# Local attention's probabilities turned by VectorE squares and a trip through device memory, instead of by TensorE transposes

## The chip, the cores and the metric

The kernel runs on one core of a Trainium2 chip. The metric is device time in microseconds of one execution. It is compared as the median of several runs.

## The reference

Two transformer blocks run on 512 tokens of width 1024, all in fp32. The change touches one piece of the first block, the local attention beside the matrix LSTM:

```python
def sliding_window_attention(q, k, v, sinks, rel_bias):
    ...
    logits = jnp.einsum('bnqhgd,bnkhd->bnhgqk', qb, kb).astype(f32) * (SWA_HEAD_DIM ** -0.5)
    ...
    mx = jnp.maximum(logits.max(-1, keepdims=True), sink)
    p = jnp.exp(logits - mx)
    probs = (p / (p.sum(-1, keepdims=True) + jnp.exp(sink - mx))).astype(v.dtype)
    out = jnp.einsum('bnhgqk,bnkhd->bnqhgd', probs, vb)
```

There are 8 heads of 64 with 2 key/value heads, and query blocks of 128 that see their own 128 keys and the 128 before (the first block sees only its own). Behind it come the output projection, cross attention over 256 memory tokens, a convolutional feed-forward net, a second block with four mixers, and its MLP.

## The kernel before

**The weights.** Every large product multiplies fp32 values split into two fp32r halves: hi by hi, lo by hi, and hi by lo, so three matmuls for one. Weights arrive in chunks of 128 x 1024 (512 KB). SyncE issues each chunk's load into one of three `stage` buffers (L2729). ScalarE casts it to `whi` (L1699), VectorE subtracts to `wlo` (L2176), and there are six places for split chunks. SyncE issues the load of chunk i+3 once VectorE has split chunk i, and the cast of a chunk waits until TensorE has used the chunk six before it.

**The order.** A class `Plan` writes the order of all steps out by hand. Every engine goes through the same list `plan.steps` and does its own part of each step, so each engine's order follows the list. `fill` takes the next free one of 8 PSUM banks, first in, first out, and `out` gives a bank back with the semaphore that frees it.

**The stage around the change.** While the first block's feature products run (`in_a`, 17 chunks, then `kv_k`, 8 chunks), small work is slipped between them by `beside_mixer_one` (L349). That is a generator: each `yield` stands for about half a chunk of feature products, 12 matmuls of 128x512 (or 24 of 128x256 further on). The local attention is cut into eight units u (two head pairs by four query blocks; units 0 and 4 have one key block, the others two), each with four heads:

- `swa_score(u)`: TensorE makes the logits in two banks (L1525). VectorE scales them, adds the bias into `L[u % 3]` (L2287), takes the negative maximum (L2291, L2293) and starts the sink's exponent (L2295).
- `swa_exp(u)`: ScalarE's exponentials with row sums (L1794). VectorE adds the sink and takes the reciprocal (L2299, L2301).
- `swa_norm(u)`: ScalarE multiplies by it (L1803).
- `swa_turn(u)`: TensorE transposes the probabilities in squares of 128x128 (L1539), 8 per unit and 4 in units 0 and 4. ScalarE copies the banks into `PTs[u % 2]` (L1814, L1816).
- `swa_pv(u)`: TensorE multiplies by the values (L1551, two records for each fp32 matmul). ScalarE copies the result to `hT` (L1821).

The mLSTM's steps follow: `ml_gate` (L1559), `ml_score` (L1566), `ml_out` (L1580). `mem_load` (L2761) loads the memory tokens, `mem_in` (L1719, L2202) splits them, and `kv_k` multiplies them. On SyncE, `mem_load` stands between the weight chunks.

## Time and profile before

| | us |
|---|---|
| median of 3 runs | 1285.17 (1284.91 to 1285.43) |
| span of the profiled execution | 1282.5 |
| TensorE busy in it | 1275.4 |
| VectorE busy | 728.4 |
| ScalarE busy | 576.5 |
| mean granted TensorE clock | 0.999 |

The span runs from the first to the last instruction of the profiled execution. That execution has no time of its own on the page, so its span is set beside the median: 2.7 us of the 1285.17 lie outside it. Busy time counts overlapping matmuls once. A matmul's duration is its latency, and the distance between two starts is what it takes from the engine.

### The profile page before, as it was taken

The page shows a single profiled execution, that of the slowest core. Times are in us where ns is not written, and L with a number is a line of the kernel's source. Part 1 is how long each engine was busy: PE and PEld are TensorE (multiplying, and loading weights), DVE is VectorE, ACT ScalarE, POOL GpSimd, SP SyncE. Part 2 cuts the span into 40 slices and gives each one's busy share as a digit, 9 for nine tenths or more (in the row PEclk, how much of TensorE's full clock was granted, in tenths as well). Part 3 has the DMA queues.
Part 4 walks back from the last instruction along what each step waited for, and adds up shares of the span by engine and source line. Part 5 has one row for each costly group of instructions (what it writes and reads, how often), then busy time and mean ns, then how long its engine had stood idle before and what let it go on. Part 6 is the DMA issues. An engine that isn't in the chain of part 4 may idle for free.

```text
span 1282.5 us, 16066 instructions
## 1 busy us (share of the span) xinstructions
PE 1275.4 (99%) x6462; PEld 1071.2 (84%) x6462; DVE 728.4 (57%) x1083; ACT 576.5 (45%) x988; POOL 7.0 (1%) x8
## 2 busy tenths in 40 slices
PE   9999999999999999999999999999999999999998
PEld 9877898898889888888888898778898888888886
DVE  5767678475576555555533489777653433433333
ACT  5577644245446444444522364576432422322222
POOL 0000001000000000000000000000000000000000
PEclk9999999999999999999999999999999999999999
DMA  8421245322234333333433142123243233333311
GB/s 257 142 78 66 99 132 157 138 54 79 82 99 132 99 99 99 99 99 99 148 99 99 33 152 92 57 66 115 64 151 93 92 97 97 115 99 99 99 50 66
DMA packets 38145, 131.20 MB, mean 102 GB/s; under 512 B 4372, under 2 KB 5908, under 8 KB 37816
## 3 DMA queue, kind: packets, MB, share of 16 engines
q1 hardware_dynamic: 37640, 129.79, 32.3%
q8 instruction: 51, 0.84, 0.3%
q10 hardware_dynamic: 432, 0.39, 0.1%
q14 instruction: 22, 0.18, 0.1%
HBM read 128.07 MB, written 2.10 MB: 101 GB/s over the span
## 4 chain that ended last, share of the span: by engine, by line
PE 99%; DMA 0%; DVE 0%; ACT 0%; issue 0%; DVEq 0%
PE bank L1283 18%; PE bank L1284 18%; PE bank L1285 18%; PE bank L1424 5%; PE bank L1425 5%; PE bank L1428 5%; PE bank L1429 5%; PE bank L1426 5%; PE bank L1427 5%; PE bank L1503 1%; PE bank L1580 1%; PE bank L1566 1%; PE bank L1366 1%; PE bank L1355 1%; PE bank L1525 1%; PE bank L1405 1%
## 5 line engine op out<-in xcount | busy, mean ns | idle before, releaser
L1283 PE MATMUL bank<-xh,whi 128*128 128x512 f32 (+1 forms) x1136 | 414.7, 365 | 0.0
L1285 PE MATMUL bank<-xh,wlo 128*128 128x512 f32 (+1 forms) x1136 | 409.9, 361 | 0.0
L1284 PE MATMUL bank<-xl,whi 128*128 128x512 f32 (+1 forms) x1136 | 409.9, 361 | 0.0
L2176 DVE TENSOR_TENSOR wlo<-stage,whi 128x1024 fp32r<-128x1024 f32 (+1 forms) x222 | 267.5, 1211 | 226.3 <-ACT whi L1699 226.1
L1699 ACT CAST whi<-stage 128x1024 fp32r<-128x1024 f32 (+1 forms) x222 | 228.5, 1036 | 198.1 <-PE bank L1429 157.1
L1283 PEld LDWEIGHTS bank<-xh,whi 128*128 128x128 f32 x1136 | 214.4, 189 | 37.6 <-issue 5.5
L1285 PEld LDWEIGHTS bank<-xh,wlo 128*128 128x128 f32 x1136 | 214.4, 189 | 32.8
L1284 PEld LDWEIGHTS bank<-xl,whi 128*128 128x128 f32 x1136 | 214.5, 189 | 31.7 <-issue 0.2
L1424 PE MATMUL bank<-whi,xh 128*128 128x512 f32 x281 | 110.3, 393 | 0.1
L1425 PE MATMUL bank<-whi,xh 128*128 128x512 f32 x281 | 109.4, 389 | 0.0
L1429 PE MATMUL bank<-whi,xl 128*128 128x512 f32 x281 | 109.4, 389 | 0.0
L1426 PE MATMUL bank<-wlo,xh 128*128 128x512 f32 x281 | 109.4, 389 | 0.0
L1427 PE MATMUL bank<-wlo,xh 128*128 128x512 f32 x281 | 109.3, 389 | 0.0
L1428 PE MATMUL bank<-whi,xl 128*128 128x512 f32 x281 | 109.3, 389 | 0.0
L2702 DVE TENSOR_TENSOR R<-bank,R 128x512 f32<-128x512 f32 x32 | 22.1, 692 | 90.7 <-ACT R L2145 90.7
L2145 ACT ACTIVATE R<-bank 128x512 f32<-128x512 f32 x32 | 19.1, 598 | 113.4 <-PE bank L1285 113.4
L2508 DVE SCALAR_TENSOR_TENSOR R<-R,par 128x512 f32<-128x512 f32 x44 | 33.1, 752 | 60.5 <-ACT R L1937 60.5
L1934 ACT COPY R<-bank 128x512 f32<-128x512 f32 x44 | 25.8, 587 | 83.7 <-PE bank L1285 83.7
L1424 PEld LDWEIGHTS bank<-whi,xh 128*128 128x128 f32 x281 | 52.8, 188 | 11.1 <-issue 0.5
L1427 PEld LDWEIGHTS bank<-wlo,xh 128*128 128x128 f32 x281 | 52.8, 188 | 11.1
L1428 PEld LDWEIGHTS bank<-whi,xl 128*128 128x128 f32 x281 | 52.7, 188 | 11.0
L1429 PEld LDWEIGHTS bank<-whi,xl 128*128 128x128 f32 x281 | 52.8, 188 | 10.9
(341 smaller groups left out, 1413.0 us busy)
## 6 DMA issues: line engine op xcount, KB each, us to landing
stage<-in_W_m SPq DMA_DIRECT2D x64, 512.0 KB, 3.6
stage<-in_W_up SPq DMA_DIRECT2D x44, 512.0 KB, 3.6
stage<-in_W_down SPq DMA_DIRECT2D x22, 512.0 KB, 3.6
stage<-in_W_in_a SPq DMA_DIRECT2D x19, 512.0 KB, 4.1
stage<-in_W_out SPq DMA_DIRECT2D x16, 512.0 KB, 3.7
stage<-in_W_in_b SPq DMA_DIRECT2D x10, 512.0 KB, 3.6
stage<-in_W_kv_k SPq DMA_DIRECT2D x8, 512.0 KB, 3.3
stage<-in_W_kv_v SPq DMA_DIRECT2D x8, 512.0 KB, 4.1
```

Source lines behind the costliest of these rows:

```text
L1283: e.matmul(b[:, cols], hi[:, k, :], xh[:, k, cols], start=(k == 0), stop=False)
L1284: e.matmul(b[:, cols], hi[:, k, :], xl[:, k, cols], start=False, stop=False)
L1285: last = e.matmul(b[:, cols], lo[:, k, :], xh[:, k, cols], start=False, stop=(k == 7))
L1424: e.matmul(b[0][:], a_hi, hi[:, 0:512], start=(k == 0), stop=False)
L1425: e.matmul(b[1][:], a_hi, hi[:, 512:1024], start=(k == 0), stop=False)
L1426: e.matmul(b[0][:], a_hi, lo[:, 0:512], start=False, stop=False)
L1427: e.matmul(b[1][:], a_hi, lo[:, 512:1024], start=False, stop=False)
L1428: e.matmul(b[0][:], a_lo, hi[:, 0:512], start=False, stop=end)
L1429: return e.matmul(b[1][:], a_lo, hi[:, 512:1024], start=False, stop=end)
L1699: e.copy(whi[:, plan.place[i], 0:width(i)], stage[:, s, 0:width(i)]).then_inc(S["w_hi"])
L2176: e.tensor_tensor(wlo[:, plan.place[i], c], stage[:, i % NSTAGE, c], whi[:, plan.place[i], c].bitcast(F32), ALU.subtract).then_inc(S["w_lo"])
L2508: e.scalar_tensor_tensor(out=y, in0=u[:, 0:512], scalar=P("fcw", w), in1=y, op0=ALU.mult, op1=ALU.add).then_inc(own.inc())
```

## The change

The transposes leave TensorE. In their place VectorE turns each unit's probabilities in squares of 32x32 (one instruction per unit, from `L` into row 2 of `gb`, in which keys four apart come to stand side by side). SyncE stores the 128x1024 (128x512 in units 0 and 4) to a scratch tensor in device memory, waits until the store has landed, waits for the values' product of the unit two before, and loads it back into `PTs[u % 2]` with runs of 1 KB (512 B in units 0 and 4), which puts the squares into place. ScalarE's copies from PSUM go. The values' product reads its moving operand in runs of 32 elements. The fills of PSUM banks by `swa_turn` go, and several steps move in the list:

```diff
-SWA_BANKS = [1, 2, 2, 2, 1, 2, 2, 2]
...
+        self.step("swa_turn", 4)
         self.step("swa_exp", 5)
         yield
-        self.swa_turn(4)
         self.step("swa_norm", 5)
+        self.swa_score(6)
+        yield
+
         self.swa_pv(3)
-        self.swa_score(6)
-        yield
-
+        self.step("swa_turn", 5)
         self.step("swa_exp", 6)
         yield
-        self.swa_pv(4)
         self.step("swa_norm", 6)
         self.swa_score(7)
         yield
 
-        self.swa_turn(5)
+        self.swa_pv(4)
+        self.step("swa_turn", 6)
         self.step("swa_exp", 7)
         yield
         self.step("swa_norm", 7)
         yield
-
-        self.swa_turn(6)
+        self.step("swa_turn", 7)
         self.step("mem_load")
         self.ml_gate(0)
         yield
+        self.swa_pv(5)
         self.step("ml_exp", 0)
         yield
 
-        self.swa_pv(5)
+        self.ml_score(0)
+        yield
         self.swa_pv(6)
-        self.swa_turn(7)
-        self.ml_score(0)
-        yield
-        yield
-
-        self.swa_pv(7)
+        yield
+
         self.ml_gate(1)
         yield
         self.step("ml_exp", 1)
         self.ml_out(0)
         yield
 
+        self.swa_pv(7)
         self.ml_score(1)
```

On TensorE the values' product changes:

```diff
-                q.wait_ge(S["swa_pt"], sum(SWA_BANKS[:u + 1]))
+                q.wait_ge(s_turned[u % 2], 16 * (u // 2 + 1))
                 q.wait_ge(S["sv_out"], 4)
                 kbs = [0, 1] if n else [1]
-                for kb in kbs:
+                P = swa_turned(u)
+                for z, kb in enumerate(kbs):
                     for j in range(2):
                         last = e.matmul(b[64 * j:64 * j + 64, 0:256], swv[:, n - 1 + kb, 64 * j:64 * j + 64],
-                                        PTs[u % 2][:, j, kb, :], start=(kb == kbs[0]), stop=(kb == 1))
+                                        P[:, j, z, :, :, :], start=(kb == kbs[0]), stop=(kb == 1))
...
+        def swa_turned(u):
+
+            k = 2 if u % 4 else 1
+            v = PTs[u % 2][:, 0:512 * k]
+            return v.rearrange("p (b j i k c) -> p j k i b c", b=4, j=2, i=2, k=k)
```

New on VectorE (first) and on SyncE (second):

```diff
+            def swa_turn(u):
+
+                q.wait_ge(S["swa_p"], u + 1)
+                if u:
+                    q.wait_ge(S["swa_out"], 16 * u)
+                else:
+                    q.wait_ge(S["gate_h"], 1)
+                    q.wait_ge(S["gate_l"], 2)
+                m = 8 if u % 4 else 4
+                src = L[u % 3].rearrange("p g (k a r) -> p r g k a", k=2, r=4)
+                dst = blocks[:, 0:128 * m]
+                if m == 8:
+                    e.transpose(dst.rearrange("p (r g k a) -> p r g k a", r=4, g=4, k=2), src).then_inc(S["swa_tr"])
+                else:
+                    e.transpose(dst.rearrange("p (r g a) -> p r g a", r=4, g=4), src[:, :, :, 1, :]).then_inc(S["swa_tr"])
...
+            def swa_turn(u):
+                w = 1024 if u % 4 else 512
+                q.wait_ge(S["swa_tr"], u + 1)
+                e.dma_start(turned[u][:, 0:w], blocks[:, 0:w]).then_inc(S["swa_out"], 16)
+                q.wait_ge(S["swa_out"], 16 * u + 16)
+                if u >= 2:
+                    q.wait_ge(S["swa_o_full"], u - 1)
+                e.dma_start(PTs[u % 2][:, 0:w].rearrange("p (b c) -> p b c", b=4),
+                            turned[u][:, 0:w].rearrange("(b a) (r c) -> (a r) b c", b=4, r=4)).then_inc(s_turned[u % 2], 16)
```

Waits elsewhere for the transposes (`swa_t_full`) now wait for VectorE's squares (`swa_tr`), and `ml_out(0)` on VectorE no longer waits for the last values' product.

How the instructions move, at three places. On TensorE, before, around unit 3's product (L1539 transposes, L1551 values' product, L1525 scores; each x4 of L1551 is one unit with two key blocks, x2 one with one, and between the groups stand the feature products, L1283 to L1285):

```order
L1285 MATMUL bank<-xh,wlo 128x512
L1539 MATMUL bank<-ident,R 128x128 x4
L1551 MATMUL bank<-R 64x256 x4
L1525 MATMUL bank<-R 128x256 x4
L1283 MATMUL bank<-xh,whi 128x512
...
L1551 MATMUL bank<-R 64x256 x2
L1525 MATMUL bank<-R 128x256 x4
L1283 MATMUL bank<-xh,whi 128x512
```

Now (L1527 scores, L1540 values' product, L1285 to L1287 features):

```order
L1527 MATMUL bank<-R 128x256 x4
L1285 MATMUL bank<-xh,whi 128x512
...
L1540 MATMUL bank<-R 64x256 x4
L1285 MATMUL bank<-xh,whi 128x512
...
L1527 MATMUL bank<-R 128x256 x4
L1285 MATMUL bank<-xh,whi 128x512
...
L1540 MATMUL bank<-R 64x256 x2
```

Twelve feature matmuls stand between each of these and the next: the group of unit 4's transposes, unit 3's product and unit 6's scores has become two groups, with no transposes, and so has unit 4's product with unit 7's scores.

On VectorE, before, between the scores of unit 2 and the next conv, with the semaphores that each waits for:

```order
L2293 TENSOR_TENSOR st<-st,gb 128x4 [waits v_own]
L2295 TENSOR_TENSOR st<-gb,st 128x4 [waits swa_nm]
L2318 SCALAR_TENSOR_TENSOR R<-R 128x512 [waits qk_t]
L2176 TENSOR_TENSOR wlo<-stage,whi 128x1024 [waits w_hi,st0]
L2299 TENSOR_TENSOR st<-st 128x4 [waits swa_e]
```

Now:

```order
L2270 TENSOR_TENSOR st<-st,gb 128x4 [waits v_own]
L2272 TENSOR_TENSOR st<-gb,st 128x4 [waits swa_nm]
L2292 STREAM_TRANSPOSE gb<-R 128x1024 [waits swa_out,swa_p]
L2311 SCALAR_TENSOR_TENSOR R<-R 128x512 [waits qk_t]
L2153 TENSOR_TENSOR wlo<-stage,whi 128x1024 [waits w_hi,st2]
L2276 TENSOR_TENSOR st<-st 128x4 [waits swa_e]
```

Unit 1's squares stand behind unit 2's logits and ahead of a silu and a chunk's split. On SyncE, before:

```order
L2729 DMA stage<-in_W_in_a 128x1024 [waits w_lo] x10
L2729 DMA stage<-in_W_kv_k 128x1024 [waits w_lo] x6
L2761 DMA R<-in_memT 128x2048 [waits swa_s_full]
```

Now, from the last units on:

```order
L2760 DMA turned<-gb 128x1024
L2764 DMA R<-turned 128x4x256
L2723 DMA stage<-in_W_kv_k 128x1024
L2760 DMA turned<-gb 128x1024
L2764 DMA R<-turned 128x4x256
L2755 DMA R<-in_memT 128x2048
L2723 DMA stage<-in_W_kv_k 128x1024 x2
```

Sixteen transfers stand between the weight chunks, the last two directly ahead of the memory tokens' load.

## Rows read from the trace of the kernel before

**Rows 1.** The page: busy us of each engine, its share of the span and its instructions.
```profile
PE 1275.4 (99%) x6462; PEld 1071.2 (84%) x6462; DVE 728.4 (57%) x1083; ACT 576.5 (45%) x988; POOL 7.0 (1%) x8
```

**Rows 2.** The longest of TensorE's waits (engine line <- releaser: us in total, times, longest us).
```profile
PE bank L1678 <- DVE R L2224: 1.2, 1, 1.2
```

**Rows 3.** TensorE's timeline (start us, us, engine, line, ...), around unit 1's transposes.
```profile
78.63 0.39 PE L1285 MATMUL bank<-xh,wlo 128*128 128x512 f32 x1
78.86 1.03 PE L1539 MATMUL bank<-ident,R 128*128 128x128 f32 x8
79.65 0.48 PE L1283 MATMUL bank<-xh,whi 128*128 128x512 f32 x1
79.97 0.40 PE L1284 MATMUL bank<-xl,whi 128*128 128x512 f32 x1
```

**Rows 4.** TensorE's timeline, around the transposes of units 0 and 4.
```profile
68.92 0.60 PE L1539 MATMUL bank<-ident,R 128*128 128x128 f32 x4
69.59 0.40 PE L1284 MATMUL bank<-xl,whi 128*128 128x512 f32 x1
...
112.13 0.60 PE L1539 MATMUL bank<-ident,R 128*128 128x128 f32 x4
112.66 1.08 PE L1551 MATMUL bank<-R 128*64 128x256 f32 x8
```

**Rows 5.** TensorE's timeline, units 5 and 6's products, unit 7's transposes.
```profile
138.48 1.95 PE L1551 MATMUL bank<-R 128*64 128x256 f32 x16
140.36 1.09 PE L1539 MATMUL bank<-ident,R 128*128 128x128 f32 x8
141.29 2.32 PE L1566 MATMUL bank<-R 128*128 128x512 f32 x8
```

**Rows 6.** TensorE's timeline, in and out of a short group between feature products.
```profile
149.08 0.28 PE L1285 MATMUL bank<-xh,wlo 128*128 128x256 f32 x1
149.29 1.08 PE L1551 MATMUL bank<-R 128*64 128x256 f32 x8
...
150.73 0.38 PE L1283 MATMUL bank<-xh,whi 128*128 128x256 f32 x1
150.95 0.28 PE L1284 MATMUL bank<-xl,whi 128*128 128x256 f32 x1
```

**Rows 7.** Groups by form (xcount | busy us, mean ns | idle before).
```profile
L1539 PE MATMUL bank<-ident,R 128*128 128x128 f32 x56 | 7.5, 273 | 0.0
...
L2291 DVE TENSOR_REDUCE st<-R 128x4 f32<-128x1024 f32 x6 | 7.3, 1220 | 0.2
```

**Rows 8.** Timelines: unit 1 normed, unit 2's logits done, product 1; the latter for product 0.
```profile
70.04 1.71 ACT L1803 ACTIVATE R<-R,st 128x256 f32<-128x256 f32 x4
...
78.58 0.17 DVE L2295 TENSOR_TENSOR st<-gb,st 128x4 f32<-128x4 f32 x1
...
93.51 1.08 PE L1551 MATMUL bank<-R 128*64 128x256 f32 x8
...
66.24 0.16 DVE L2295 TENSOR_TENSOR st<-gb,st 128x4 f32<-128x4 f32 x1
...
82.56 0.65 PE L1551 MATMUL bank<-R 128*64 128x256 f32 x4
```

**Rows 9.** DMA issues (xcount, KB each, median us from issue to landing).
```profile
stage<-in_W_in_a SPq DMA_DIRECT2D x19, 512.0 KB, 4.1
...
R<-in_x SPq DMA_DIRECT2D x4, 512.0 KB, 7.4
...
out<-R SPq DMA_DIRECT2D x3, 512.0 KB, 2.6
```

**Rows 10.** Window of the squares: PE, PEld, DVE, ACT, POOL busy (x), clock, DMA share, GB/s.
```profile
66.40:134.40 68.00, 68.00 (x353) 52.27 (x352) 45.27 (x80) 49.60 (x131) 0.00 (x0) 1.00 0.22 70
```

**Rows 11.** Timelines: the memory tokens' cast, the group ahead of their first product.
```profile
146.58 2.00 ACT L1719 CAST xh<-R 128x1024 fp32r<-128x1024 f32 x2 [4.45 <-PE bank L1285]
...
153.71 2.40 PE L1580 MATMUL bank<-R 128*128 128x129 f32 x20
```

More of the change, by code:

```diff
@@ L308, in swa_score @@
         self.step("swa_score", u)
-    def swa_turn(self, u):
-        for z in range(SWA_BANKS[u]):
-            self.fill("swa_turn", u, z)
-            self.out(("swa_turn", u, z), "swa_pt", sum(SWA_BANKS[:u]) + z + 1)
-        self.step("swa_turn", u)
     def swa_pv(self, u):
@@ L361, in beside_mixer_one @@
         yield
+        self.step("swa_turn", 0)
         self.step("swa_exp", 1)
         yield
-        self.swa_turn(0)
         self.step("swa_norm", 1)
@@ L370, in beside_mixer_one @@
         yield
+        self.step("swa_turn", 1)
         self.step("swa_exp", 2)
         yield
-        self.swa_turn(1)
         self.step("swa_norm", 2)
@@ L379, in beside_mixer_one @@
         yield
+        self.step("swa_turn", 2)
         self.step("swa_exp", 3)
         yield
-        self.swa_turn(2)
         self.step("swa_norm", 3)
@@ L389, in beside_mixer_one @@
         yield
+        self.step("swa_turn", 3)
         self.step("swa_exp", 4)
         yield
-        self.swa_turn(3)
         self.step("swa_norm", 4)
@@ L1141, in build_program @@
         L = [tiles(reg(kb, 1024), 4) for kb in (24, 72, 68)]
-        PTs = [reg(76 + 4 * i, 1024).rearrange("p (j k c) -> p j k c", j=2, k=2) for i in range(2)]
+        PTs = [reg(76 + 4 * i, 1024) for i in range(2)]
+        blocks = gb[:, 2, :]
+        s_turned = [S["swa_in0"], S["swa_in1"]]
         vaug = reg(84, 2064).rearrange("p (t h c) -> p t h c", t=4, h=4)
@@ L1263, in bank_of @@
             return bank[plan.bank[key][0]]
+        turned = [nc.dram_tensor(f"turned{u}", (128, 1024 if u % 4 else 512), F32, kind="Internal").ap() for u in range(8)]
         block = ctx.enter_context(nc.Block())
@@ L1527, in swa_score @@
                 last.then_inc(S["swa_s_full"])
-            def swa_turn(u):
-                n = u % 4
-                q.wait_ge(S["ld_c"], 32)
-                q.wait_ge(S["swa_p"], u + 1)
-                for j in range(2):
-                    if j < SWA_BANKS[u]:
-                        b = fill("swa_turn", u, j)
-                    for kb in ([0, 1] if n else [1]):
-                        a = kb * 256 if n else j * 256
-                        for i in range(2):
-                            last = e.transpose(b[:, a + 128 * i:a + 128 * i + 128], L[u % 3][:, 2 * j + i, tok(kb)], ident[:])
-                    if j or SWA_BANKS[u] == 2:
-                        last.then_inc(S["swa_t_full"])
             def swa_pv(u):
@@ L1804, in swa_norm @@
                 last.then_inc(S["swa_p"])
-            def swa_turn(u):
-                m = sum(SWA_BANKS[:u])
-                if u >= 2:
-                    q.wait_ge(S["swa_o_full"], u - 1)
-                for z in range(SWA_BANKS[u]):
-                    q.wait_ge(S["swa_t_full"], m + z + 1)
-                    b = bank_of("swa_turn", u, z)
-                    if SWA_BANKS[u] == 2:
-                        e.copy(PTs[u % 2][:, z, :, :], tiles(b[:], 2)).then_inc(S["swa_pt"])
-                    else:
-                        e.copy(PTs[u % 2][:, :, 1, :], tiles(b[:], 2)).then_inc(S["swa_pt"])
             def swa_pv(u):
@@ L1846, in ml_exp @@
                 q.wait_ge(S["ml_d"], h + 1)
-                q.wait_ge(S["swa_t_full"], sum(SWA_BANKS[:6 + 2 * h]))
+                q.wait_ge(S["swa_tr"], min(8, 6 + 2 * h))
                 if h >= 2:
@@ L1867, in kv_v @@
                 q.wait_ge(S["qk_s"], 8)
-                q.wait_ge(S["swa_t_full"], sum(SWA_BANKS))
+                q.wait_ge(S["swa_tr"], 8)
                 e.copy(VM[:, t, hf * 512:(hf + 1) * 512], bank_of("kv_v", hf, t)[:]).then_inc(S["vm_out"])
@@ L2282, in swa_score @@
                 if u >= 3:
-                    q.wait_ge(S["swa_t_full"], sum(SWA_BANKS[:u - 2]))
+                    q.wait_ge(S["swa_tr"], u - 2)
                 q.wait_ge(S["swa_s_full"], u + 1)
@@ L2354, in ml_out @@
                 q.wait_ge(S["ml_h_full"], h + 1)
-                q.wait_ge(S["swa_t_full"], sum(SWA_BANKS))
-                q.wait_ge(S["swa_o_full"], 8)
+                q.wait_ge(S["swa_tr"], 8)
+                if h:
+                    q.wait_ge(S["swa_o_full"], 7)
                 for z in range(2):
@@ L2810, in _ @@
                 x_load(k)
-            mine = dict(begin=begin, bias_load=bias_load, split=split, x_in=x_in, consts=consts, mem_load=mem_load, x_again=x_again, rows=rows, mix2_loads=mix2_loads, store=store)
+            mine = dict(begin=begin, bias_load=bias_load, split=split, x_in=x_in, consts=consts, mem_load=mem_load, swa_turn=swa_turn, x_again=x_again, rows=rows, mix2_loads=mix2_loads, store=store)
             for name, *a in plan.steps:
```

18 lines of the change are left out of this document (9 added, 9 removed).

## Prediction

> **What bounds the kernel now.** I read the page's busy shares first, then TensorE's waits, then the timelines of the stretch in which the local attention runs. TensorE is busy for 1275.4 of the 1282.5 us of the span [rows 1], and its longest wait is 1.2 us, once, at the start [rows 2]. So TensorE's own instruction stream is the time, and every other engine is cover. Only two things can move the time: an instruction that leaves or joins that stream, or a wait that did not exist. The span stands 2.7 us under the median of 1285.17; I take the differences below as the same in both.
>
> **What leaves TensorE.** The transposes are listed with 273 ns each [rows 7]. That is a latency: the eight of unit 1 start at 78.86 and the next product starts at 79.65, so they take 0.79 us, 0.1 each. The first product behind them takes 0.32 us to the next start instead of the usual 0.23 (78.63 to 78.86), so a lone group of eight costs 79.97 - 78.86 - 0.23 = 0.88 us [rows 3]. Units 1, 2, 3, 5 and 6 are of this kind: 5 x 0.88 = 4.4 us. Unit 0 (four transposes): 69.59 - 68.92 - 0.23 = 0.44 us. Unit 4 stands ahead of a values' product: 112.66 - 112.13 = 0.53 us, less the 0.09 us that a product behind feature matmuls pays to get in (149.08 + 0.12 = 149.20, start at 149.29 [rows 6]), so 0.44 [rows 4]. Unit 7, in the middle of a group: 141.29 - 140.36 = 0.93 us [rows 5]. Sum removed: 4.4 + 0.44 + 0.44 + 0.93 = 6.2 us.
>
> The Trainium skill, "TensorE: Matmul & The Clock Gate", section "Part 4: PE-mode transpose", gives a transpose about 275 ns in a kernel. The trace's duration agrees (273), but its starts are 0.1 us apart, and the starts decide; by 275 ns each the sum would be 15 us.
>
> **What the reordering adds to TensorE.** Each short group between feature products costs 0.09 us to get in and 0.10 to get out (150.73 to 150.95 is 0.22 where a half product takes 0.12) [rows 6]. The groups on transposes alone go, and that is in the sum above. But product 3 now stands apart from scores 6, product 4 from scores 7, and the large group of products 5 and 6 with the first mLSTM scores becomes three. That is four groups more: 4 x 0.19 = 0.8 us. Product 7 only changes the group that it is part of.
>
> **The values' product itself** keeps its number of records and columns, but reads its moving operand in runs of 32 elements instead of 128. No row shows such an operand. The trace's product reads contiguous columns: 16 records take 1.88 us (138.48 to 140.36 [rows 5]) and 8 take about 1.0 with the change of kind behind them, so one is 0.11 us. Bounds: 0 if runs of 32 stream as well, and 56 x 0.11 = +6.2 us if they halve the rate. I take 0, nearest to the contiguous row, because the elements still lie side by side for 32 starts in a row.
>
> **Sum:** -6.2 + 0.8 = -5.4 us, to 1279.8.
>
> **What must be hidden for that.** Three pieces of new work lie on engines that are cover now.
>
> *VectorE* gets eight square turns, six of 1024 columns. No row shows a transpose there. The nearest row by size is the reduce over 1024 columns, 1.22 us [rows 7]. Lower end: half of that, 0.6 us; upper end: double, 2.4 us, because the source is read with a stride of four elements. I take 1.2 for 1024 columns and 0.7 for 512, so 8.6 us in all; at the upper end it is 17. In the window in which they fall VectorE is busy for 45.3 of 68.0 us [rows 10], so 22.7 us are idle, and both fit. ScalarE loses 14 copies in the same window. The turn waits for ScalarE's norm, but that is early: for unit 1 it ends at 71.75, and VectorE comes to the place of the turn at 78.75, behind unit 2's logits [rows 8]. What queues behind the turn is a silu, a chunk's split and the next reciprocal. They come 1.2 us later, and a chunk is split six places ahead of its use.
>
> The Trainium skill, "SBUF — State Buffer", section "Door 1: The DMA port swizzle", says that compute engines read 16-byte lines and pay for each step to another line; here every source element is on a new line. That rule speaks for the upper end, and for the product's runs of 32, which use every line fully, it speaks for 0. No run here has shown either.
>
> *The trip.* The product of unit u must find both transfers done. Unit 1 is the tightest. VectorE reaches the turn at 78.75 and TensorE reaches product 1 at 93.51 [rows 8], 14.8 us later. The transposes of units 1 and 2 leave TensorE in between (-1.8), and the turn takes 1.2, so 11.8 us are left for store and load. Unit 0 has 82.56 - 66.40 = 16.2, less 1.3 and 0.7, so 14.1; units 2 and 4 come out near 14 in the same way, and the rest, whose products moved back or which have a free yield, above 15. The nearest rows: a store of 512 KB lands in 2.6 us, and a load of 512 KB in 4.1 among the weight chunks; the slowest load of that size took 7.4, behind others [rows 9]. So the pair is 6.7 us and at most 2 x 7.4 = 14.8. By 6.7 nothing waits, with 5 us to spare at unit 1. By 14.8 unit 1 waits 3.0 us and units 0, 2 and 4 about 0.7 each: +5.
>
> *SyncE's queue.* SyncE waits for each store to land before it goes on, and the weight chunks stand behind it. It loses the store's 2.6 us (at most 7.4) per unit, while a chunk's load is issued three chunks ahead of its cast. A chunk is 24 products of 0.23 us, 5.5 us, so the lead is 16 us less 4.1 to land: 12 us. It holds. The last pair stands ahead of the memory tokens' load. Their cast waits for TensorE until 146.58, and their first product comes after the group at 153.71 [rows 11], so the load can be some 5 us late without cost. The extra bytes are under 7 MB in a window with a DMA share of 0.22 [rows 10].
>
> **Rivals.**
>
> *A. The trip is too long (slower).* The products 0 to 7 wait in TensorE's stream for a load whose store first has to land in device memory. It decides from a pair of 11.8 us on. Because everything hangs on TensorE, a wait does not give the next unit more room. At 18 us units 1, 0, 2 and 4 wait 6.2, 3.9, 3.8 and 3.9 us, and the other four about 2 each: 26 us, to 1306; at 16 us it is about 10 us, to 1290. SyncE's chunks starve from the same point. For it: each unit has two transfers in a row, with a wait on SyncE between, and the load is cut into runs of 1 KB, which no row of that size shows. Against it: the rows of 2.6 and 4.1 us. I give 0.08, at 1290.
>
> *B. Small waits.* The pair is 12 to 15 us at one or two units, or VectorE at 2.4 us per turn comes late to a bank or a split. TensorE waits 1 to 5 us: 1281 to 1285. For it: VectorE and ScalarE work in step here and each late piece is passed on. I give 0.10.
>
> *C. The strided operand halves the product's rate.* +6.2 us on the forecast, 1286.0: the gain is spent where it was made. Chance 0.06.
>
> *D. The listed duration is what a transpose costs.* Then 56 x 0.273 = 15.3 us leave, less 0.8: 1270.7. Against it are the starts of rows 3, 0.1 us apart. Chance 0.02. It is also the time by the skill's 275 ns.
>
> **How the numbers follow.** A measurement of this kernel tells a change of 0.2% (2.6 us) from none, so faster is below 1282.6. My forecast, 1279.8, has 0.74, and a range of its own from 1278.0 (the split groups cost nothing and the removed transposes leave all of the 6.2 us, with a run's spread) to 1281.5. B adds 0.10 up to 1284.8. So the range of 1278.0 to 1284.8 holds 0.84 and leaves out A, C and D. Faster: 0.74, D's 0.02 and half of B, so 0.81. Same: the other half of B and C, which ends 0.8 us above the time before, so 0.11. Slower: A, 0.08.
>
> **What would show it.** In the changed profile TensorE has 56 transpose records fewer on the attention's line and, if I am right, no wait of its own at the values' product. The product's records still start 0.11 us apart inside a group (0.22 would be C). A square turn on VectorE lasts near 1.2 us (2.4 is the stride's price). Store and load together land within 7 us of the turn's end and SyncE's chunks still wait for VectorE's splits. The prediction is wrong if TensorE waits for a load of `PTs`, or for a bank or a split in the stretch from 65 to 160 us, by more than 1 us in all, or if the time changes anywhere behind that stretch, where no instruction has changed.

## The result, and the profile after

The change makes the kernel faster: median 1281.45 us (1280.76 to 1281.67, 7 runs) against 1284.98 (1284.82 to 1285.43, 7 runs) for the kernel before, a ratio of 0.997 with a 95% interval of 0.9961 to 0.9979. That is 3.5 us where 5.4 were forecast. It lies inside the range and on the side that was forecast; 1.9 us of the gain are missing.

The page of the kernel after: its span, each engine's busy time (as [rows 1]) and the chain that ended last, by engine.

```profile
span 1279.3 us, 15979 instructions
PE 1271.2 (99%) x6406; PEld 1065.5 (83%) x6406; DVE 740.7 (58%) x1091; ACT 569.1 (44%) x974; POOL 7.0 (1%) x8
PE 92%; DVE 4%; ACT 2%; DMA 1%; issue 1%; DVEq 0%; SPq 0%
```

TensorE has 56 records fewer and is busy for 4.2 us less than in [rows 1]; the span is 3.2 us shorter. What TensorE waited for (us in total, times, longest us), as [rows 2], says where some of the gain went:

```profile
PE bank L1667 <- DVE R L2201: 1.2, 1, 1.2
PE bank L1285 <- DVE xl L2179: 0.9, 1, 0.9
PE bank L1322 <- ACT xh L1695: 0.2, 1, 0.2
```

The first is the wait that was there before. The second is new: the first product of the memory tokens (L1285) waits for VectorE's split of them (L2179). No wait for `PTs` at the values' product (L1540) is listed. The same list for TensorE's weight loads (PEld) has, beside the same wait for the split, one at 157.63 for a PSUM bank that VectorE gives back with its work on the mLSTM outputs (L2363):

```profile
PEld bank L1285 <- DVE R L2363: 0.5, 1, 0.5
```

(A third, of 0.35 us at 121.54, is no longer than the gap that weight loads have ahead of such a group in any case.) The kernel before has no wait for another engine in the attention's stretch.

The square turns and one TensorE form, by source line (xcount, shortest, median and longest ns, first and last start, form):

```profile
L2292 DVE STREAM_TRANSPOSE gb<-R x6: 1983/2005/2054, 78.5 to 133.9; 128x1024 f32<-128x1024 f32 x6
...
L2294 DVE STREAM_TRANSPOSE gb<-R x2: 1080/1086/1093, 68.5 to 110.3; 128x512 f32<-128x512 f32 x2
...
L1540 PE MATMUL bank<-R x56: 379/379/430, 81.7 to 154.8; 128*64 128x256 f32 x56
```

A turn takes 2.0 us, nearer the upper bound of 2.4 than the 1.2 taken. The values' product keeps its duration, and eight of its records still take 1.08 us [rows 6], so runs of 32 elements cost it nothing.

The trip's transfers in the list of DMA issues (xcount, KB each, median us from issue to landing), beside [rows 9]:

```profile
turned<-gb SPq DMA_DIRECT2D x6, 512.0 KB, 3.1
R<-turned SPq DMA_DIRECT2D x6, 512.0 KB, 3.9
...
turned<-gb SPq DMA_DIRECT2D x2, 256.0 KB, 3.4
R<-turned SPq DMA_DIRECT2D x2, 256.0 KB, 2.7
```

So a store and a load take 7.0 us in the median, near the 6.7 of the sum.

**Where the time is.** I compare starts of the same TensorE groups, counted from the first scores, because the start-up ahead of them differs from one execution to the next (52.41 us before, 52.91 after; more on this below). Up to the first mLSTM output group (L1580, 153.71 before [rows 11]; L1569, 147.72 after), TensorE is (153.71 - 52.41) - (147.72 - 52.91) = 6.49 us ahead. Product 7, 1.02 us, now stands behind that point, so 5.47 us have been gained there: the forecast's 5.4. Behind it the gain shrinks. TensorE's timeline after (start us, us, engine, line):

```profile
147.72 2.40 PE L1569 MATMUL bank<-R 128*128 128x129 f32 x20
...
151.01 0.39 PE L1285 MATMUL bank<-xh,whi 128*128 128x256 f32 x1 [0.89 <-DVE xl L2179]
...
154.07 1.08 PE L1540 MATMUL bank<-R 128*64 128x256 f32 x8
155.09 2.42 PE L1555 MATMUL bank<-R 128*128 128x512 f32 x8
```

What stood in front of that wait, on ScalarE and then on VectorE:

```profile
147.44 1.99 ACT L1708 CAST xh<-R 128x1024 fp32r<-128x1024 f32 x2 [5.69 <-DMA R<-in_memT]
```
```profile
132.71 1.23 DVE L2153 TENSOR_TENSOR wlo<-stage,whi 128x1024 fp32r<-128x1024 f32 x1 [0.32 <-ACT whi L1688]
133.86 2.05 DVE L2292 STREAM_TRANSPOSE gb<-R 128x1024 f32<-128x1024 f32 x1
...
148.59 2.36 DVE L2179 TENSOR_TENSOR xl<-R,xh 128x1024 fp32r<-128x1024 f32 x2 [3.92 <-ACT xh L1708]
```

And SyncE's queue, the first line from the kernel before, the others after:

```profile
134.85 0.43 SPq L2761 DMA_DIRECT2D R<-in_memT  x1
```
```profile
131.81 0.37 SPq L2764 DMA_DIRECT2D R<-turned  x1
133.97 0.33 SPq L2723 DMA_DIRECT2D stage<-in_W_kv_k  x1
135.94 0.32 SPq L2760 DMA_DIRECT2D turned<-gb  x1
140.86 0.37 SPq L2764 DMA_DIRECT2D R<-turned  x1
141.28 0.51 SPq L2755 DMA_DIRECT2D R<-in_memT  x1
```

Read backwards: the product at 151.01 waited for VectorE's split, which waited for ScalarE's cast, which had stood idle for 5.69 us until the memory tokens' load landed at 147.4. Before, the same cast was held up by TensorE instead ([rows 11]). The load was issued at 141.28, because SyncE first waited for unit 7's store: issued at 135.94, right behind unit 7's turn (133.86 + 2.05), and waited for until 140.86, 4.9 us. In the kernel before, the load was issued at 134.85.

The second wait follows from the first. VectorE splits the memory tokens from 148.59 on, where e1_mem_first below has it do so from 145.45 on, so its work on the mLSTM outputs comes late too. The second piece of it ends at 157.22 + 0.35 = 157.57, and the next feature product starts at 157.63, 2.54 us behind the start of the mLSTM scores instead of 2.08.

### The profile page after: what moved, and what is told of

Read it like the earlier page. It is cut to its first block, busy times and chain, and to the rows that moved or that the text cites. A ratio compares the mean times of both kernels' runs of the same rounds, so it can differ in the third digit from the quotient of the medians.

```text
span 1279.3 us, 15979 instructions
## 1 busy us (share of the span) xinstructions
PE 1271.2 (99%) x6406; PEld 1065.5 (83%) x6406; DVE 740.7 (58%) x1091; ACT 569.1 (44%) x974; POOL 7.0 (1%) x8
## 2 busy tenths in 40 slices
DMA packets 43521, 138.54 MB, mean 108 GB/s; under 512 B 4628, under 2 KB 10260, under 8 KB 43192
## 4 chain that ended last, share of the span: by engine, by line
PE 92%; DVE 4%; ACT 2%; DMA 1%; issue 1%; DVEq 0%; SPq 0%
PE bank L1285 16%; PE bank L1286 16%; PE bank L1287 16%; PE bank L1426 5%; PE bank L1427 5%; PE bank L1429 5%; PE bank L1430 5%; PE bank L1428 5%; PE bank L1431 5%; PE bank L1505 1%; DVE wlo L2153 1%; DVE R L2302 1%; PE bank L1357 1%; PE bank L1368 1%; DVE gb L2292 1%
## 5 line engine op out<-in xcount | busy, mean ns | idle before, releaser
L1285 PE MATMUL bank<-xh,whi 128*128 128x512 f32 (+1 forms) x1136 | 414.6, 365 | 1.0 <-DVE xl L2179 0.9
L1287 PE MATMUL bank<-xh,wlo 128*128 128x512 f32 (+1 forms) x1136 | 409.9, 361 | 0.0
L1285 PEld LDWEIGHTS bank<-xh,whi 128*128 128x128 f32 x1136 | 214.4, 189 | 40.8 <-issue 7.0
L1287 PEld LDWEIGHTS bank<-xh,wlo 128*128 128x128 f32 x1136 | 214.4, 189 | 32.5
L1429 PEld LDWEIGHTS bank<-wlo,xh 128*128 128x128 f32 x281 | 52.7, 188 | 11.1
L1428 PEld LDWEIGHTS bank<-wlo,xh 128*128 128x128 f32 x281 | 52.8, 188 | 11.1
L1431 PEld LDWEIGHTS bank<-whi,xl 128*128 128x128 f32 x281 | 52.7, 188 | 11.0
```

What stands on the lines that cost most here:

```text
L1285: e.matmul(b[:, cols], hi[:, k, :], xh[:, k, cols], start=(k == 0), stop=False)
L1287: last = e.matmul(b[:, cols], lo[:, k, :], xh[:, k, cols], start=False, stop=(k == 7))
L1428: e.matmul(b[0][:], a_hi, lo[:, 0:512], start=False, stop=False)
L1429: e.matmul(b[1][:], a_hi, lo[:, 512:1024], start=False, stop=False)
L1431: return e.matmul(b[1][:], a_lo, hi[:, 512:1024], start=False, stop=end)
```

## The experiments

I call the explanation so far theory L: the load of the memory tokens stands behind unit 7's trip and lands too late; that costs the wait and the lateness behind it. Its rivals: VectorE's longer turns cost the time in themselves, by making later pieces late; the groups that the new order splits off cost more than the 0.19 us that the sum counts for each; the trips hold up SyncE's weight chunks. The number that I compare in each is the *stretch*, from the first scores to the start of the last group of mLSTM transposes (L1587 before, L1576 after), because it leaves out the start-up: 220.61 - 52.41 = 168.20 us before and 217.38 - 52.91 = 164.47 after. Of the 5.47 us gained at 147.72, 3.73 are left there. Its two ends, before and then after:

```profile
52.41 0.71 PE L1525 MATMUL bank<-R 64*128 64x128 f32 x8
...
220.61 0.60 PE L1587 MATMUL bank<-ident,R 128*128 128x128 f32 x4
```
```profile
52.91 0.72 PE L1527 MATMUL bank<-R 64*128 64x128 f32 x8
...
217.38 0.60 PE L1576 MATMUL bank<-ident,R 128*128 128x128 f32 x4
```

Behind the stretch nothing changed: the stretch is 3.7 us shorter, and the 0.5 us more in front of it leave the 3.2 us between the spans. Each stretch is read from the one profiled execution of its kernel.

**e1_mem_first: the memory tokens' load ahead of the last trip.**

```diff
-        self.step("swa_turn", 7)
         self.step("mem_load")
+        self.step("swa_turn", 7)
         self.ml_gate(0)
```

> The change, with the memory tokens' load issued on SyncE ahead of unit 7's store and load instead of behind them; nothing else moves. Theory L (of the forecast's 5.4 us, some 1.6 are lost because that load is issued 6 us late, behind a store that SyncE waits for): TensorE's 0.9 us wait at the first kv_k product goes and so does the half microsecond that follows in the first mLSTM score group behind it; 1.4 to 1.8 us less than the change, near 1279.8. Rival V (VectorE's turns of 2.0 us instead of 1.2 are what is late, and the load only stands there): at most 0.3 us less. Rival N (the half microsecond by which this execution is behind before the attention begins is part of the change, not spread): the start of the first scores stays at 52.9 here too; as spread it varies between 52.4 and 52.9.

Measured: 1280.45 us (1280.10 to 1280.75) against 1284.79 for the kernel before, ratio 0.9964 (0.995 to 0.9977). TensorE's waits no longer name the split:

```profile
PE bank L1667 <- DVE R L2201: 1.2, 1, 1.2
PE bank L1322 <- ACT xh L1695: 0.2, 1, 0.2
```

The load is issued at 135.20 and the stretch is 162.92 us, 5.28 less than before and 1.55 less than in the change. Product 7 starts 5.20 us behind the mLSTM output group instead of 6.35, and the group behind it lasts 8.11 us to the next anchor instead of 8.49. The turns still take 2.01 us. So the late load cost 1.15 us directly and 0.4 behind it, and the wait of the weight load for VectorE's bank is gone as well. This separates L from the rival on the turns, which expected at most 0.3 us. The length of the turns by itself costs nothing where the load does not hang on the last of them. The median gained only 4.3 us because this kernel's first scores start at 53.77 in the profiled execution, 1.36 us later than before: 5.28 - 1.36 is the 3.9 us between the spans (1282.5 and 1278.6).

**e2_contiguous_turn: the turn reads neighbouring elements.** ScalarE's copy of the keys, the bias and the mask put the keys in turned order, so that the square turn has no stride of four at its source.

```diff
-                e.copy(swk if j == 0 else swq[:, int(MIX1[j][2]), :], bank_of("in_a", j)[:]).then_inc(S["a_out"])
+                e.copy(swk.rearrange("p (t r a) -> p t a r", t=4, r=4) if j == 0 else swq[:, int(MIX1[j][2]), :],
+                       bank_of("in_a", j)[:].rearrange("p (t a r) -> p t a r", t=4, r=4) if j == 0 else bank_of("in_a", j)[:]
+                       ).then_inc(S["a_out"])
...
-                src = L[u % 3].rearrange("p g (k a r) -> p r g k a", k=2, r=4)
+                src = L[u % 3].rearrange("p g (k r a) -> p r g k a", k=2, r=4)
...
-    r, c = np.arange(128)[:, None], np.arange(256)[None, :]
+    r, c = np.arange(128)[:, None], np.arange(256).reshape(2, 32, 4).transpose(0, 2, 1).reshape(1, 256)
```

> The change, with the keys put in the turned order once, when ScalarE copies them from PSUM (and the bias and mask laid out so on the host), so that the square turn reads 32 elements side by side instead of a stride of four. If the stride is the price of the turn (2.0 us for 1024 columns), it falls to about 1.1; if a turn of fp32 costs that whatever the stride, it stays at 2.0. For the time: V expects 1.4 to 1.8 us less. L expects the same only as far as the last turn, and with it the memory tokens' load, comes earlier: one turn alone gives 0.9 us of the 1.1 us lost directly, several turns together more. If the duration stays, both expect no change.

Measured: 1280.08 us (1279.68 to 1280.65), ratio 0.9961 (0.9948 to 0.9973); stretch 162.93. The turn in the groups by form (xcount | busy us, mean ns | idle us before), first of e1_mem_first, whose source has the stride, then of e2_contiguous_turn:

```profile
L2292 DVE STREAM_TRANSPOSE gb<-R 128x1024 f32<-128x1024 f32 x6 | 12.1, 2012 | 0.0
...
L2294 DVE STREAM_TRANSPOSE gb<-R 128x512 f32<-128x512 f32 x2 | 2.2, 1081 | 0.0
```
```profile
L2294 DVE STREAM_TRANSPOSE gb<-R 128x1024 f32<-128x1024 f32 x6 | 7.4, 1239 | 0.0
...
L2296 DVE STREAM_TRANSPOSE gb<-R 128x512 f32<-128x512 f32 x2 | 1.4, 702 | 0.0
```

Without the stride a turn takes 1.24 us for 1024 columns and 0.70 for 512, just what the sum took (1.2 and 0.7). The stride costs 0.77 us per large turn. With turns that short the load of the memory tokens is issued at 140.28 instead of 141.28, and TensorE's wait is gone too. The last store is issued 2.2 us earlier (133.76 instead of 135.94), but it then takes 6.1 us instead of 4.9 (to 139.86), so only 1.0 us of that reaches the load. So the turn's length did cost time, by one way alone: through the load behind unit 7. This and e1_mem_first end at the same stretch, which speaks for one cause and not for two.

**e3_order_only: the new order, with TensorE's transposes kept.** From the kernel before, with the products at the change's places, and the wait of `ml_out(0)` on VectorE cut to match:

```diff
         self.swa_turn(4)
         self.step("swa_norm", 5)
-        self.swa_pv(3)
         self.swa_score(6)
         yield
+        self.swa_pv(3)
         self.step("swa_exp", 6)
         yield
-        self.swa_pv(4)
         self.step("swa_norm", 6)
         self.swa_score(7)
         yield
+        self.swa_pv(4)
         self.swa_turn(5)
...
         self.ml_gate(0)
         yield
+        self.swa_pv(5)
         self.step("ml_exp", 0)
         yield
-        self.swa_pv(5)
-        self.swa_pv(6)
         self.swa_turn(7)
         self.ml_score(0)
         yield
+        self.swa_pv(6)
         yield
-        self.swa_pv(7)
         self.ml_gate(1)
...
         self.ml_out(0)
         yield
+        self.swa_pv(7)
         self.ml_score(1)
...
-                q.wait_ge(S["swa_o_full"], 8)
+                if h:
+                    q.wait_ge(S["swa_o_full"], 7)
```

> The kernel before, with TensorE's transposes and ScalarE's copies kept, but the values' products at the places of the change (3 behind scores 6, 4 behind scores 7, 5, 6 and 7 apart). By the forecast's term each group more among the feature products costs 0.19 us; here there are three more (eight become eleven), so +0.6 us against the kernel before, within 0.2. If a group costs nothing, 0; if the moved products wait for something, over 1 us, and a wait of TensorE is listed.

Measured: 1285.99 us (1285.49 to 1286.98, 11 runs) against 1284.79, ratio 1.0008 (1.0 to 1.0017); stretch 169.19, 0.99 more than before. So the new order by itself gains nothing; it costs about 1 us of the stretch. Here it splits off three groups (product 4 stays with unit 5's transposes), so 3 x 0.19 = 0.6 us of the 0.99 were counted. Some 0.1 us is product 7 in its new group (8.11 us to the next anchor instead of 7.99), and 0.3 us stay unexplained; no wait is listed.

**e4_trip_on_gpsimd: GpSimd issues the trips.** SyncE's part of `swa_turn` moves word for word to GpSimd, in a loop over the eight units, so that SyncE waits for no store.

```diff
+            for u in range(8):
+                swa_turn(u)
             for h in range(4):
...
-            mine = dict(begin=begin, bias_load=bias_load, split=split, x_in=x_in, consts=consts, mem_load=mem_load, swa_turn=swa_turn, x_again=x_again, rows=rows, mix2_loads=mix2_loads, store=store)
+            mine = dict(begin=begin, bias_load=bias_load, split=split, x_in=x_in, consts=consts, mem_load=mem_load, x_again=x_again, rows=rows, mix2_loads=mix2_loads, store=store)
```

> The change, with the store and load of the turned squares issued by GpSimd instead of SyncE, so that no weight chunk and not the memory tokens' load stands behind them. L expects the load to be issued near 134 us instead of 141, TensorE's 0.9 us wait to go, and 1.4 to 1.8 us less than the change, unless GpSimd's transfers take over 4 us longer than SyncE's, when a product of the values waits (0 to 3 us more). V expects at most 0.3 us less.

Measured: 1280.05 us (1279.58 to 1280.26), ratio 0.996 (0.9948 to 0.9973); stretch 162.92. The memory tokens' load is issued at 134.79, the wait is gone, and a store and a load take 3.1 and 4.3 us in the median. All that this edit frees beyond e1_mem_first is the weight chunks' loads, and the stretch is the same to 0.01 us: SyncE's chunks were never short.

**e5_mem_first_contiguous: both edits, e1's and e2's.**

```diff
-        self.step("swa_turn", 7)
         self.step("mem_load")
+        self.step("swa_turn", 7)
...
-                src = L[u % 3].rearrange("p g (k a r) -> p r g k a", k=2, r=4)
+                src = L[u % 3].rearrange("p g (k r a) -> p r g k a", k=2, r=4)
...
```

> Both mends at once: the memory tokens' load ahead of unit 7's trip, and the contiguous square turn. If the late load was all that was lost, the second mend has nothing left to give: the same as either alone within 0.2 us in the stretch from the first scores on, 1280.1 to 1280.5. If VectorE's time still costs TensorE something that no listed wait shows, another 0.5 us or more less.

Measured: 1280.10 us (median of five runs, 1279.08 to 1280.20; a sixth took 5816 us and is left out), ratio 0.9959 (0.9946 to 0.9972). The stretch is 162.92 us, as with either edit alone, although the load is now issued at 132.07. Two cures of one wait do not add up.

**e6_mem_first_store_twice: a longer trip, with the load out of its way.** From e1_mem_first, with each store made twice, one behind the other.

```diff
-                q.wait_ge(S["swa_out"], 16 * u + 16)
+                q.wait_ge(S["swa_out"], 32 * u + 16)
+                e.dma_start(turned[u][:, 0:w], blocks[:, 0:w]).then_inc(S["swa_out"], 16)
+                q.wait_ge(S["swa_out"], 32 * u + 32)
```

> The memory tokens' load first, and every unit's squares stored twice, the second store waiting for the first: each trip is one store longer, by about 3.1 us. In the trace of the change the loads land 3.8 to 9 us before their product (nearest for units 2 and 5). The forecast's term (a trip costs TensorE nothing below its slack) expects at most 0.5 us more than with the memory load alone first. Rival A (the trip is what TensorE hangs on) expects 8 times 3 us, 20 us or more.

Measured: 1280.42 us (1279.85 to 1281.50), ratio 0.9964 (0.9952 to 0.9975); stretch 163.69, 0.77 more than e1_mem_first. One wait appears, at product 7:

```profile
PE bank L1540 <- DMA R<-turned: 0.5, 1, 0.5
```

That is 0.3 us more than the 0.5 expected at most. Seven of the eight units still wait for nothing, although from the issue of the first store to the landing of the load they now take about 8 to 11 us. Unit 7's first store stands behind the memory tokens' load of 1 MB and takes 9.4 us by itself (138.00 to 147.41), and its trip some 16. So trips of that length cost nothing here, as the prediction said with its room of 11.8 us. The 16 and 18 us at every unit that rival A was priced for were not reached, so this run says nothing on its price.

**e8_store_twice: the same on the change itself**, with the memory tokens' load left behind the last trip. The diff is e6's, on the kernel after.

> The change with every unit's squares stored twice and the memory tokens' load left behind unit 7's trip. L expects that load, and TensorE's wait for it, to come about 3 us later: 3 to 3.5 us more than the change, near 1284.8, all of it at the first kv_k product. Without that place (the run with the memory load first) the same doubling should cost nothing.

Measured: 1287.32 us (1286.13 to 1288.32, 11 runs) against 1285.18, ratio 1.0018 (1.001 to 1.0027): slower than the kernel before. The stretch is 171.49 us, 7.0 more than the change, about twice what was expected. TensorE's wait for the split has grown from 0.9 to 6.0 us:

```profile
PE bank L1285 <- DVE xl L2179: 6.0, 1, 6.0
```

The last unit's two stores took 6.4 and 2.6 us (SyncE went on 143.24 - 136.85 and 145.82 - 143.24 later), and the load went out at 146.57 instead of 141.28. That is 5.3 later, and the wait is 5.1 longer; it agrees. The rest comes from the clock. Windows of TensorE around the wait, the busy time of PE, PEld, DVE, ACT and POOL (x instructions), the granted clock, the DMA share and GB/s:

```profile
149.90:155.90 6.00, 0.01 (x1) 0.00 (x0) 2.39 (x3) 3.54 (x5) 0.00 (x0) 0.87 0.46 188
155.90:158.00 2.10, 2.08 (x9) 2.08 (x10) 2.03 (x4) 2.08 (x6) 0.00 (x0) 0.50 0.00 0
158.00:160.00 2.00, 2.00 (x11) 2.00 (x11) 2.00 (x3) 2.00 (x7) 0.00 (x0) 0.50 0.00 0
160.00:162.00 2.00, 2.00 (x15) 1.60 (x14) 1.79 (x9) 0.80 (x1) 0.00 (x0) 0.72 0.17 35
162.00:164.00 2.00, 2.00 (x9) 0.97 (x6) 1.75 (x8) 0.00 (x0) 0.00 (x0) 1.00 0.61 236
```

After 6.0 us without work the granted clock is at 0.50, the 1.2 GHz level, until some time between 160 and 162 us. From the first product behind the wait to product 7, TensorE takes 5.35 us here and 3.06 in the change: 2.3 us on top of the wait. Behind product 7 it is 0.4 us faster than the change (62.92 us to the end of the stretch instead of 63.31): VectorE has caught up, and the wait for its bank is gone. 5.1 + 2.3 - 0.4 are the 7.0 us.

**e7_merged_groups: the split groups put together again.** From e5_mem_first_contiguous: product 3 with scores 6, 4 with 7, 5 with the first mLSTM scores, 6 with the second gate.

```diff
+        self.swa_pv(3)
         self.swa_score(6)
         yield
-        self.swa_pv(3)
...
+        self.swa_pv(4)
         self.swa_score(7)
         yield
-        self.swa_pv(4)
...
-        self.swa_pv(5)
         self.step("ml_exp", 0)
         yield
+        self.swa_pv(5)
         self.ml_score(0)
         yield
-        self.swa_pv(6)
         yield
+        self.swa_pv(6)
         self.ml_gate(1)
```

> Both mends, and the values' products put back into groups: 3 with scores 6, 4 with scores 7, 5 with the first mLSTM scores, 6 with the second gate. Four groups fewer among the feature products at 0.19 us each: 0.8 us less than both mends, near 1279.3, if the loads are there in time. Product 4 then stands 4 us earlier, with about 1 us of slack left; if it waits, up to 1 us of that is given back.

Measured: 1280.11 us (1279.15 to 1281.28), ratio 0.9959 (0.9947 to 0.9971); stretch 163.36, 0.44 more than e5_mem_first_contiguous. Product 4 now stands half a chunk and a group of scores earlier, and gets there 1.0 us before its load has landed:

```profile
PE bank L1540 <- DMA R<-turned: 1.0, 1, 1.0
```

Without that 1.0 us the four merges would have gained 0.56, 0.14 each.

**e9_merged_but_4: the same without the merge of product 4.**

> Both mends and the merged groups, but product 4 left where the change has it, behind scores 7. In the run with all groups merged product 4 waited 1.0 us for its load; without that wait the stretch from the first scores on would have been 0.6 us shorter than with both mends. Here no wait of TensorE, and 0.4 to 0.6 us less than both mends in that stretch; in the medians that is within their spread.

Measured: 1279.79 us (1279.03 to 1280.21) against 1285.05, ratio 0.9955 (0.9942 to 0.9969). The values' product waits for nothing, and the stretch is 162.50, 0.42 less than e5_mem_first_contiguous for three merges, again 0.14 each.

**e10_one_leg: no scratch memory.** All four merges, and four transfers from SBUF to SBUF per unit in place of the store and the load, each one reading 32 partitions and writing 128. Nothing waits for a store any more, and the next turn waits for these transfers instead.

```diff
-                e.dma_start(turned[u][:, 0:w], blocks[:, 0:w]).then_inc(S["swa_out"], 16)
-                q.wait_ge(S["swa_out"], 16 * u + 16)
                 if u >= 2:
                     q.wait_ge(S["swa_o_full"], u - 1)
-                e.dma_start(PTs[u % 2][:, 0:w].rearrange("p (b c) -> p b c", b=4),
-                            turned[u][:, 0:w].rearrange("(b a) (r c) -> (a r) b c", b=4, r=4)).then_inc(s_turned[u % 2], 16)
+                for b in range(4):
+                    e.dma_start(PTs[u % 2][:, b * w // 4:(b + 1) * w // 4],
+                                blocks[32 * b:32 * b + 32, 0:w].rearrange("a (r c) -> a r c", r=4)).then_inc(s_turned[u % 2], 16)
```

> All groups merged, both mends, and no scratch tensor: four transfers per unit, one for each 32 partitions of the turned squares, go from SBUF straight into place, so that SyncE waits for no store. If two legs are what made product 4 late, its load now lands 3 us earlier or more, the 1.0 us wait goes, and the stretch is 0.6 us shorter than with both mends, at or below the run with product 4 left apart. If a transfer from 32 partitions to 128 in runs of 1 KB is much slower than a load (over 7 us), product 4 waits as before or longer.

Measured: 1278.91 us (1278.73 to 1279.71) against 1285.05, ratio 0.9952 (0.9939 to 0.9964), the fastest of all. The transfers in the list of DMA issues:

```profile
R<-gb SPq DMA_DIRECT2D x24, 128.0 KB, 2.8
...
R<-gb SPq DMA_DIRECT2D x8, 64.0 KB, 2.7
```

SyncE takes 2.5 us to issue a unit's four, and the last lands some 3 us behind its issue, so the trip takes about 5 us, 2 less than by device memory. The wait of 1.0 us at product 4 is gone and the stretch is 162.29, 0.63 less than e5_mem_first_contiguous: four merges at 0.16. By the stretch this beats the kernel before by 5.9 us, and the change by 2.2.

## Why the prediction was right, and where it failed

**The time** came out inside the range, at its upper end: 1281.45 where 1281.5 bounds the forecast's own range. What that rests on is mixed: the sum was right, and a part of the cover was not.

**The sum** holds as a whole. Removed 6.2, added 0.8, so -5.4: measured 5.47 us at the last anchor ahead of the new wait, and -5.28 over the whole stretch once the wait is gone (e1_mem_first, e2_contiguous_turn, e4_trip_on_gpsimd and e5_mem_first_contiguous all within 0.01 us). Its two terms are each a few tenths too large, and that they cancel is luck. With the four groups merged again and no wait (e10_one_leg), the stretch is 5.91 us shorter than before: that is what the transposes took, against 6.2. The four groups then took 0.63, against 0.8. The transposes' cost was read from their starts and not from their durations, and this decides against rival D: by 273 ns each, 15 us would have left. The Trainium skill's figure of about 275 ns ("TensorE: Matmul & The Clock Gate", "Part 4: PE-mode transpose") holds for the duration of one alone.

**A split group** was priced at 0.19 us. Measured backwards, by merging, it is 0.14 to 0.16; in the order alone three splits cost 0.99 us, of which 0.3 stay unexplained. For the sum this is a matter of 0.2 us, or more if the unexplained part belongs to the groups.

**The values' product** on runs of 32 elements was taken at no cost. That is right (379 ns, eight in 1.08 us), and rival C is dismissed.

**The trip** was right in its length, 7.0 us against 6.7, and in that no product waits. The units' loads landed between 3.8 and 9 us ahead of their products; at unit 1 it was 4.6, where the forecast had 5. But unit 1 was not the tightest: units 2 and 5 had 3.8. For unit 5 the forecast had over 15 us left for store and load, and it was 11.4 (119.74 to 131.14). The extra bytes were 7.3 MB (138.54 less 131.20 MB of DMA packets) and not under 7; nothing hung on that.

**SyncE's chunks** were right: no chunk was late (e4_trip_on_gpsimd).

**The step that failed** stands at the end of the same paragraph on SyncE's queue: the memory tokens' load "can be some 5 us late without cost". The place and the mechanism were seen, and the room comes out about right (140.4 - 134.85 = 5.5 us), in part by luck. The forecast took it from the old timetable, in which the load lands 5.4 us behind its issue, at 140.25, and TensorE holds up the cast until 146.58. In the new one the limit is the product itself, which TensorE now reaches at 150.12 instead of 155.86, and which happens to need the load by about 146.5 as well. The lateness was never worked out, and by the forecast's own sizes it would have come out harmless. From the last turn's start to the load's issue they give 1.2 (turn) + 2.6 (store) + 0.4 (issue) = 4.2 us. Measured are 2.05 + 4.92 + 0.42 = 7.4: the load is issued at 141.28 and lands at 147.4. TensorE came to the product 0.89 us before the split was ready, so the load had to land by about 146.5. With 4.2 us it would have been issued at 138.1 and landed, 6.1 later, at 144.2, in time. Two terms were mis-sized.

- *The turn*, 2.0 us and not 1.2. The sum took the row of the reduce over the estimate for the stride, though both stood there. The Trainium skill's rule on 16-byte lines ("SBUF — State Buffer", "Door 1: The DMA port swizzle") had spoken for the upper end, and e2_contiguous_turn agrees with it in direction: 2.01 us with each element on a line of its own, 1.24 with neighbours, a factor of 1.6.
- *The last store*, 4.9 us and not 2.6. The row for 2.6 was an output store with nothing ahead of it. This one is issued 2 us behind a 512 KB weight chunk and 4 behind unit 6's load. The range's other end for it, 7.4, would have shown the trouble; it was tried on the products and not on what stands behind the last trip. The two terms are not independent: in e2_contiguous_turn the shorter turns brought this store forward by 2.2 us, and it took 1.2 us longer. What sets a store's time was not taken apart; the rows show only that it grows with what was issued just ahead of it.

A third thing works against the load: just before VectorE comes to the last turn, TensorE is 4.5 us ahead of its old times (the same feature product starts at 130.60 instead of 135.06), and VectorE only 0.5 us ahead (its split ahead of the turn starts at 132.71 instead of 133.23). The gain of the change itself brings the use of the load forward, while the load's own chain does not move with it.

The time lies where rival B, with 0.10, had put it (1281 to 1285), but B's two mechanisms are not what happened: the pair of transfers stayed at 7.0 us, and VectorE did not come late to the split of the memory tokens, it stood idle for 3.92 us before it. The one bank that it gave back late was late through the load as well. The prediction had set "more than 1 us" of waits for a load, a bank or a split between 65 and 160 us as the sign of being wrong, and by that sign it was wrong: 0.9 us for the split and about 0.4 for the bank, and 1.5 us of the stretch were lost. Its other sign did not appear: behind 160 us nothing changed.

**Rival A** was rightly small: it began at a pair of 11.8 us, and 7.0 were measured. But its sign was not foreign to this kernel: e8_store_twice, with stores of twice the length, is slower than the kernel before. It became so at the place that failed here and by the clock, not at the products, where A had put it. What trips of 16 us at every unit would cost was not measured.

**What stays open.** The medians gained less than the stretches (e1_mem_first: 4.3 and 5.3 us), because the start-up ahead of the first scores was longer in most changed kernels. First scores start at 52.41 in the kernel before, 52.91 in the change, 52.46 to 54.16 in the experiments. Most of that arises in the first 7 us. TensorE's first products, in the kernel before, then in e1_mem_first, and then products of about the same size in e8_store_twice, where the granted clock was 0.50:

```profile
5.40 0.40 PE L1320 MATMUL bank<-wlo,xh 128*128 128x264 f32 x2
5.64 0.40 PE L1320 MATMUL bank<-whi,xl 128*128 128x264 f32 x2
```
```profile
5.80 0.64 PE L1322 MATMUL bank<-whi,xh 128*128 128x264 f32 x2
6.25 0.64 PE L1322 MATMUL bank<-wlo,xh 128*128 128x264 f32 x2
```
```profile
156.94 0.41 PE L1286 MATMUL bank<-xl,whi 128*128 128x256 f32 x1
157.16 0.41 PE L1287 MATMUL bank<-xh,wlo 128*128 128x256 f32 x1
```

Two of e1_mem_first's products take 0.45 us, so each takes about 0.22, as in e8_store_twice; in the kernel before two take 0.24. The views list a clock of 1.00 there, but they count time without a clock record as full, and the traces' first clock record begins 4.1 us into the span in the kernel before, 4.2 in the change, 7.3 in e1_mem_first and 7.4 in e7_merged_groups, the kernel with the latest first scores. So the longer start-up is most likely TensorE at the lower of its two levels, at work without a pause, for up to 3 us longer. That was read off the traces and not tested. It does not cover the 0.5 us by which the change itself starts its first scores later, and whether the change adds those was not tried. The runs of the kernel before alone are spread over 1284.28 to 1286.14 us.

## What to carry to other kernels

When a step with a wait is put on a queue, work out when each thing behind its last instance is issued and needed, in the new timetable and with the upper bound of every unknown duration; here that was one load, and a swap of two lines gave back 1.5 us of the stretch (1.0 in the medians). Take the cost of short TensorE instructions from the distance of their starts. Two cures of one wait don't add, and a good experiment applies each alone before it applies both.

## What the runs showed of the hardware

- A square turn of 128x1024 fp32 on VectorE takes 1.24 us with neighbouring source elements and 2.01 with a stride of four; 128x512 takes 0.70 and 1.08.
- A store of 512 KB, alone in 2.6 us [rows 9], took 4.9 behind a weight chunk and a load, and 6.4 in e8_store_twice, issued 2.1 us behind unit 6's load and 1.7 behind a chunk. Behind the memory tokens' load of 1 MB it took 7.5 us in e1_mem_first and 9.4 in e6_mem_first_store_twice. That load landed in 6.1 us in the change, in 7.8 in e1_mem_first and in 9.1 in e5_mem_first_contiguous, where unit 7's trip follows it in the queue.
- After 6.0 us of idle TensorE the granted clock was 0.50 for over 4 us of full work, which cost 2.3 us more. In the change, the listed clock stayed at 1.00 from 149 to 160 us, with the 0.9 us of idle time in it.
- The first 12 products of the stage ahead of the first scores span 1.6 us in the kernel before and 2.8 us in e1_mem_first, and the clock record of the latter begins 3.2 us later.
